# One-hot matmuls for the first gather and the last combine of a routed expert layer, and row numbers made in a copied last body

## The chip, the cores and the metric

The kernel runs on one NeuronCore of a Trainium2 chip. The metric is the device time of one execution in microseconds (us), lower is better. Five engines work side by side, each through its own list of instructions: TensorE (PE; its weight loads are shown apart as PEld), VectorE (DVE), ScalarE (ACT), GpSimd (POOL) and SyncE (SP, which only issues transfers). They meet at semaphores.

## What is computed

A two-layer transformer trunk over 256 tokens of width 1024, all in float32: attention, memory cross-attention and a feed-forward part in each layer, every one followed by `x = LayerNorm(ALPHA * x + part(x))`. The change touches only the last feed-forward part, a mixture of 8 experts of inner width 3584, of which each token takes the best two:

```python
def moe_swiglu(x, router, w_gate, w_up, w_down):
    logits = (x @ router).astype(jnp.float32)
    top_vals, top_idx = lax.top_k(logits, TOP_K)          # TOP_K = 2
    gates = jax.nn.softmax(top_vals, axis=-1)
    combine = jnp.sum(one_hot(top_idx, N_EXPERTS) * gates[..., None], axis=-2)
    y = jnp.zeros_like(x)
    for e in range(N_EXPERTS):                             # 8
        y = y + combine[..., e:e + 1] * swiglu(x, w_gate[e], w_up[e], w_down[e])
    return y
h = layer_norm(ALPHA * h + moe_swiglu(...), ln_g[1, 2], ln_b[1, 2])
```

## The kernel before

**Weights in chunks.** Every weight matrix comes in chunks of 128 x 2048 floats (1 MB), issued by SP into a ring of raw tiles. ACT rounds a chunk into `w_hi` (the `copy` at L993), DVE takes the rest into `w_lo` (L1798 in the expert loop, L1344 before it), and PE multiplies with three products for each piece, `x_hi*w_hi`, `x_hi*w_lo`, `x_lo*w_hi` (L362 to L364), 12 matmuls a chunk in the expert loop. There are three slots for `w_hi` and `w_lo`: ACT may split chunk n + 3 only when PE has finished chunk n (`chunk_used`), and DVE follows ACT (`hi_made`), PE follows DVE (`lo_made`).

**The expert loop.** An expert is one job of a hardware loop on each of PE, ACT, DVE and POOL, `n_rounds * 8` jobs (one round with these inputs). A job has 42 chunks, numbered c = 0 to 41: c = 0 to 27 make, for seven column blocks j, the gate (two chunks, bank `eg`) and the up product (two chunks, bank `eu`); c = 28 to 41 are the down product, in two halves of seven chunks (`ed0`, `ed1`). Beside them ACT does SiLU of a gate (L1282, at c%4 = 1), DVE multiplies it with the up product (L1790, c%4 = 3), PE transposes the result in the next block (L771), and ACT and DVE split the transposed tile (`eT_hi` at L993, `eT_lo` at L1812, c%4 = 2). ACT copies each finished half of `y` out of PSUM at c = 34 and c = 41 and issues its store to `y_rows` in HBM (L1293).

**Rows of tokens.** An expert works on at most 128 tokens. `place` holds each token's place in each expert, `pick` (L1724) is its one-hot form, 2 x 128 x 128. A matmul with `pick` makes the token numbers (L716), DVE turns them into integers (`got_i`), POOL gathers these rows of `x_rows` from HBM with an indirect transfer (L955), and PE turns the gathered tile (L726) before ACT and DVE split it into `xe_hi` and `xe_lo` (L1738). For the first expert all this stands ahead of the loop; for the next ones it is done inside the job before (index at c = 4, turn at c = 32).

**The end.** After the loop POOL gathers, for each half of the width, each of two token tiles and each of the two choices, 128 rows of `y_rows` into `y_got` (L964, 8 gathers), and DVE adds them, scaled by `g1` or `g2`, to X (L1831), makes the statistics (L1834) and does the last LayerNorm (L1837 to L1858). The row numbers for these gathers (`row_i`, L1752 to L1768), the gates (L1769 to L1771) and `X *= ALPHA` (L1778) are made by DVE ahead of the loop.

**Order.** Everything is ordered by hand: each engine runs the statements of its block in the order in which they are written, and waits block what stands behind them on the same engine.

Of the kernel before, what the change touches and what calls it, by code (L numbers as in the profile page):

```python
# [31 lines left out]
def trunk(nc, x, mem, ln_g, ln_b, mem_wq, mem_wkv, mem_wo, ab_w_in, ab_sinks, ab_w_out,  # L32
# [74 lines left out]
    with ExitStack() as ctx:  # L107
# [13 lines left out]
        def take(name, shape, dt=F32):  # L121
            size = 4
            for s in shape[1:]:
# [78 lines left out]
                   for i in range(2)] for t in range(TB)] for half in range(2)]  # L202
        raw_exp = [raw[(N0 + i) % NRAW] for i in range(NRAW)]
# [13 lines left out]
        for name, shape, dt in (  # L217
# [7 lines left out]
                ("row_i11", [P, 1], U32)):  # L225
# [10 lines left out]
            small[n] for n in ("token_no", "got_i", "mine", "nth", "late"))  # L236
        row_i = [[small[f"row_i{t}{i}"] for i in range(2)] for t in range(TB)]
# [32 lines left out]
        C_INDEX, C_TURN = 4, 4 * EJ + 4  # L270
# [71 lines left out]
        def _(pe):  # L342
# [368 lines left out]

            def index(tag, job):
# [18 lines left out]
            index("iA", None)  # L731
            pe.wait_ge(sem("x_got"), 16)
            turn("xA", None)
            pe.wait_ge(sem("rounds_made"), 1)
            n_rounds = pe.value_load(rounds[0:1, 0:1], min_val=1, max_val=2)
            before = [list(claims), list(signals)]
            with pe.Fori(0, n_rounds * NE) as job:
                start = list(claims)
                for c in range(EC):
# [4 lines left out]
                    if c == C_INDEX:  # L744
                        pe.wait_ge(sem("picked"), job + 2)
                        index("iB", job)
                    if c < 4 * EJ:
                        j, q = c // 4, c % 4
                        key, b = (f"eg{j}", j % 2) if q < 2 else (f"eu{j}", 2 + j % 2)
# [4 lines left out]
                    else:  # L754
                        i, q = divmod(c - 4 * EJ, EK // CK)
                        if q == 0:
                            claim(pe, f"ed{i}", 4 + i, job, signal=False)
                        if i == 0:

                            wait_emptied(pe, f"et{q}", job)  # L760
# [3 lines left out]
                    if c % 4 == 1 and 1 <= c // 4 <= EJ:  # L764
# [4 lines left out]
                        d = claim(pe, f"et{j}", b, job)  # L769
# [4 lines left out]
                    if c == C_TURN:  # L774

                        pe.wait_ge(sem("x_got"), 16 * job + 32)
                        turn("xB", job)
            assert [a - b for a, b in zip(claims, before[0])] == JOB_CLAIMS
            assert [a - b for a, b in zip(signals, before[1])] == JOB_SIGNALS

# [55 lines left out]
        def _(pool):  # L836
# [132 lines left out]
            pool.wait_ge(sem("y_filled"), 16 * 2 * (NE * P // SEQ))  # L969
# [3 lines left out]
            pool.wait_ge(sem("index_made"), 1)  # L973
            get_x()
            pool.wait_ge(sem("rounds_made"), 1)
# [12 lines left out]
        def _(act):  # L988
# [274 lines left out]
            with act.Fori(0, n_rounds * NE) as job:  # L1263
                for c in range(EC):
# [32 lines left out]
                    else:  # L1297
# [3 lines left out]
                        with act.Else():  # L1301
                            act.nop()
# [584 lines left out]
```

## Time and profile before

| | us |
|---|---|
| median of 3 runs | 1739.4 (1738.62 to 1739.58) |
| the profiled execution | 1737.09 |
| its span in the trace | 1735.3 |
| PE busy | 1648.1 |
| DVE busy | 1274.5 |
| ACT busy | 1069.5 |
| POOL busy | 102.9 |

The expert layer takes the second half of the span, from about 740 us on. The page says how busy each engine is; who waits for whom in a stretch is read from the timeline of that stretch, and what sets the end from the chain of work that ended last.

### The profile page before, as it was taken

The numbers are of one execution on the slowest core, as the hardware profiler recorded it, in microseconds if no ns is written. First come the engines' busy times: TensorE is split into PE (matmuls) and PEld (weight loads), VectorE is DVE, ScalarE is ACT, GpSimd is POOL, SyncE is SP. The second block draws the span as 40 slices with busy tenths as digits, with TensorE's granted clock in tenths as the row PEclk, the third lists the DMA queues.
The fourth block names the chain that finished last, engine by engine and source line by source line (L and its number), as shares of the span: only waits on it lengthen the run. The fifth ranks groups of instructions, "written<-read, shape, count | busy, mean of one in ns | idle before, by whom it ended". The sixth has DMA issues, their size and how long they took to land.

```text
span 1735.3 us, 21609 instructions
## 1 busy us (share of the span) xinstructions
PE 1648.1 (95%) x7704; PEld 1355.7 (78%) x7704; DVE 1274.5 (73%) x1080; ACT 1069.5 (62%) x951; POOL 102.9 (6%) x124
## 2 busy tenths in 40 slices
PE   7998988999999998799999999999999999999994
PEld 6787777888787787578878788788788788787883
DVE  4564746445655664588889799898898898898996
ACT  4575444434344544367777777777777777777772
POOL 2000110000101210100000000000000000000002
PEclk9998999999999999889999999999999999999997
DMA  9423915545555444389999999999999999999993
GB/s 317 169 73 121 309 56 193 182 158 194 193 185 171 131 149 143 121 287 365 376 376 374 372 374 363 376 377 371 368 380 362 381 364 377 379 360 379 373 366 108
DMA packets 238097, 480.56 MB, mean 277 GB/s; under 512 B 8224, under 2 KB 11328, under 8 KB 238048
## 3 DMA queue, kind: packets, MB, share of 16 engines
q1 hardware_dynamic: 229456, 454.06, 73.5%
q0 software_dynamic: 6288, 21.63, 4.0%
q10 hardware_dynamic: 2304, 4.20, 0.6%
q8 instruction: 32, 0.52, 0.1%
q14 instruction: 17, 0.14, 0.0%
HBM read 473.54 MB, written 10.51 MB: 279 GB/s over the span
## 4 chain that ended last, share of the span: by engine, by line
PE 81%; DVE 8%; ACT 7%; issue 3%; DMA 1%; ACTq 1%; POOL 0%; POOLq 0%; DVEq 0%
PE bank L362 25%; PE bank L364 24%; PE bank L363 24%; ACT w_hi L993 3%; DVE w_lo L1798 2%; PE bank L406 2%; DVE w_lo L1344 1%; PE bank L771 1%; PE bank L651 1%; DVE X L1381 1%; DVE X L1390 1%; ACT y L993 1%; PE bank L503 1%; PE bank L501 1%; ACT L1282 1%
## 5 line engine op out<-in xcount | busy, mean ns | idle before, releaser
L993 ACT ACTIVATE w_hi<-raw 128x2048 fp32r<-128x2048 f32 (+1 forms) x385 | 730.7, 1904 | 301.2 <-PE bank L364 286.2
L1798 DVE TENSOR_TENSOR w_lo<-raw,w_hi 128x2048 fp32r<-128x2048 f32 x285 | 647.2, 2291 | 114.1 <-ACT w_hi L993 102.3
L362 PE MATMUL bank<-w_hi,xe_hi 128*128 128x512 f32 x896 | 356.9, 398 | 5.8 <-DVE w_lo L1798 5.0
L364 PE MATMUL bank<-w_hi,xe_lo 128*128 128x512 f32 x896 | 350.2, 391 | 0.0
L363 PE MATMUL bank<-w_lo,xe_hi 128*128 128x512 f32 x896 | 349.9, 391 | 0.0
L1344 DVE TENSOR_TENSOR w_lo<-raw,w_hi 128x2048 fp32r<-128x2048 f32 (+1 forms) x95 | 210.9, 2223 | 158.6 <-ACT w_hi L993 158.4
L362 PE MATMUL bank<-w_hi,xT_hi 128*128 128x512 f32 (+1 forms) x560 | 216.8, 387 | 8.4 <-DVE w_lo L1344 5.2
L364 PE MATMUL bank<-w_hi,xT_lo 128*128 128x512 f32 (+1 forms) x560 | 214.4, 383 | 0.0
L363 PE MATMUL bank<-w_lo,xT_hi 128*128 128x512 f32 (+1 forms) x560 | 214.2, 383 | 0.0
L362 PEld LDWEIGHTS bank<-w_hi,xe_hi 128*128 128x128 f32 x896 | 168.8, 188 | 45.8 <-DVE w_lo L1798 11.5
L364 PEld LDWEIGHTS bank<-w_hi,xe_lo 128*128 128x128 f32 x896 | 168.6, 188 | 36.2
L363 PEld LDWEIGHTS bank<-w_lo,xe_hi 128*128 128x128 f32 x896 | 168.9, 189 | 33.2
L362 PE MATMUL bank<-w_hi,eT_hi 128*128 128x512 f32 x448 | 176.9, 395 | 2.2 <-DVE w_lo L1798 2.2
L364 PE MATMUL bank<-w_hi,eT_lo 128*128 128x512 f32 x448 | 174.7, 390 | 0.0
L363 PE MATMUL bank<-w_lo,eT_hi 128*128 128x512 f32 x448 | 174.4, 389 | 0.0
L362 PEld LDWEIGHTS bank<-w_hi,xT_hi 128*128 128x128 f32 x560 | 106.3, 190 | 29.6 <-issue 10.0
L364 PEld LDWEIGHTS bank<-w_hi,xT_lo 128*128 128x128 f32 x560 | 106.2, 190 | 20.7
L363 PEld LDWEIGHTS bank<-w_lo,xT_hi 128*128 128x128 f32 x560 | 106.4, 190 | 19.7
L1798 DVE TENSOR_TENSOR w_lo<-raw_more,w_hi 128x2048 fp32r<-128x2048 f32 x48 | 109.9, 2290 | 12.0 <-ACT w_hi L993 10.2
L993 ACT ACTIVATE w_hi<-raw_more 128x2048 fp32r<-128x2048 f32 x48 | 92.1, 1919 | 21.7 <-PE bank L364 21.7
L362 PEld LDWEIGHTS bank<-w_hi,eT_hi 128*128 128x128 f32 x448 | 84.1, 188 | 22.2 <-DVE w_lo L1798 5.6
L364 PEld LDWEIGHTS bank<-w_hi,eT_lo 128*128 128x128 f32 x448 | 84.1, 188 | 17.9
(264 smaller groups left out, 1617.2 us busy)
## 6 DMA issues: line engine op xcount, KB each, us to landing
raw<-in_moe_w_gate_dram SPq DMA_DIRECT2D x96, 1024.0 KB, 7.1
raw<-in_moe_w_up_dram SPq DMA_DIRECT2D x96, 1024.0 KB, 7.1
raw<-in_moe_w_down_dram SPq DMA_DIRECT2D x96, 1024.0 KB, 7.6
raw<-in_mem_wkv_dram SPq DMA_DIRECT2D x16, 1024.0 KB, 5.0
raw_more<-in_moe_w_up_dram SPq DMA_DIRECT2D x16, 1024.0 KB, 7.1
raw_more<-in_moe_w_gate_dram SPq DMA_DIRECT2D x16, 1024.0 KB, 6.6
raw_more<-in_moe_w_down_dram SPq DMA_DIRECT2D x16, 1024.0 KB, 7.8
raw<-in_c_w_in_dram SPq DMA_DIRECT2D x12, 1024.0 KB, 5.1
```

Source lines behind the costliest of these rows:

```text
L362: nc.tensor.matmul(d, xh, hi[:, k, :], start=(first and k == 0), stop=False)
L363: nc.tensor.matmul(d, xh, lo[:, k, :], start=False, stop=False)
L364: m = nc.tensor.matmul(d, xl, hi[:, k, :], start=False, stop=(last and k == n - 1))
L406: m = nc.tensor.transpose(dst[k // 2][:, c:c + P], src[:, t, k * P:(k + 1) * P], ident[:, :])
L501: nc.tensor.matmul(d[:, 0:P], qT[:, 0:P], kT[:, 0:P], start=True, stop=True, skip_group_check=True)
L503: m = nc.tensor.matmul(d[:, P:TRI], qT[:, P:SEQ], kT, start=True, stop=True, skip_group_check=True)
L651: m = nc.tensor.matmul(d[:, t * MDH:(t + 1) * MDH], PT_t[i % 2][:, mb * SEQ + t * P:mb * SEQ + (t + 1) * P], MV[:, mb, i * MDH:(i + 1) * M ...
L771: m = nc.tensor.transpose(d[:, q * P:(q + 1) * P], e_h[j % 2][:, q * P:(q + 1) * P], ident[:, :])
L993: return nc.scalar.activation(dst, src, ACT.Copy)
L1282: nc.scalar.activation(e_g[j % 2][:, :], bank_of(f"eg{j}")[:, :], ACT.Silu)\
L1344: tt(w_lo[c % NSPL][:, 0:n], raw[c % NRAW][:, 0:n], w_hi[c % NSPL][:, 0:n].bitcast(F32), ALU.subtract).then_inc(lo_made, 1)
L1798: tt(w_lo[s][:, :], raw_exp[r][:, :], w_hi[s][:, :].bitcast(F32), ALU.subtract).then_inc(lo_made, 1)
```

## The change

Five things are done.

1. **First expert's rows by matmul.** Instead of index, gather and turn ahead of the loop, PE multiplies X (still in SBUF) with `pick`: 16 matmuls of 128 columns give the transposed rows at once (`pick_rows`).
2. **The last job is a copy.** The loop runs `last = 8 * rounds - 1` jobs, and the last expert is a second, straight copy of the body (`expert(last, "z")`). The tests on the last three chunks' splits go away.
3. **Last expert's result by matmul.** In the copy PE transposes `pick` (c = 4), DVE copies it to `pickT` (c = 5), and PE multiplies it with `y` half by half (`combine`, after c = 37 and after c = 41); DVE adds that to X from PSUM (`add_last`). The last expert's `y` isn't stored. The eight gathers from HBM now concern only the other experts: they are issued as soon as the last but one expert is stored and the row numbers are made, and DVE adds them at c = 12, 16, 20 and 24 (`add_got`). A token's share from the last expert gets weight 0 there and its gate in `w_fin`.
4. **Row numbers, gates and `X *= ALPHA`** move from ahead of the loop into the copy, at c = 2 and c = 6.
5. **SiLU's table** is loaded by ACT at the top of every expert, by hand.

The core of the diff:

```diff
+        C_GOT = {12 + 4 * n: (n // TB, n % TB) for n in range(2 * TB)}
+        C_INDEX, C_TURN, C_COMBINE = 4, 4 * EJ + 4, 4 * EJ + EK // CK + 2
# TensorE
+            def pick_rows(tag):
+                for half in range(2):
+                    d = claim(pe, f"{tag}{half}", half)
+                    for q in range(4):
+                        k = 4 * half + q
+                        for t in range(TB):
+                            m = nc.tensor.matmul(d[:, q * P:(q + 1) * P], X[:, t, k * P:(k + 1) * P],
+                                                 pick[:, t, :], start=(t == 0), stop=(t == 1),
+                                                 skip_group_check=True)
+                    m.then_inc(filled[half], 1)
             pe.wait_ge(sem("picked"), 1)
-            index("iA", None)
-            pe.wait_ge(sem("x_got"), 16)
-            turn("xA", None)
-            with pe.Fori(0, n_rounds * NE) as job:
+            pick_rows("xA")
+            def combine(half, job):
+                for t in range(TB):
+                    d = claim(pe, f"c{half}{t}", 2 * half + t, job)
+                    if t == 0:
+                        pe.wait_ge(sem(f"y_made{half}"), job + 1)
+                    nc.tensor.matmul(d[:, :], pickT[:, t * P:(t + 1) * P], y[:, half * W:(half + 1) * W],
+                                     start=True, stop=True, skip_group_check=True)\
+                        .then_inc(filled[2 * half + t], 1)
+            def expert(job, z):
                     if c == C_INDEX:
                         pe.wait_ge(sem("picked"), job + 2)
-                        index("iB", job)
+                        if z:
+                            d = claim(pe, "pT", 5, job)
+                            for t in range(TB):
+                                m = nc.tensor.transpose(d[:, t * P:(t + 1) * P], pick[:, t, :], ident[:, :])
+                            m.then_inc(filled[5], 1)
+                        else:
+                            index("iB", job)
-                    if c == C_TURN:
+                    if c == C_TURN and not z:
                         turn("xB", job)
+                    if z and c in (C_COMBINE, EC - 1):
+                        if c == C_COMBINE:
+                            pe.wait_ge(sem("pickT_made"), 1)
+                        combine(int(c == EC - 1), job)
+            with pe.Fori(0, last) as job:
+                expert(job, "")
+            expert(last, "z")
# GpSimd
-                        for r in range(NE * P, 2 * NE * P, SEQ):
+                        for r in range((NE - 2) * P, 2 * NE * P, SEQ):
-            pool.wait_ge(sem("index_made"), 1)
-            get_x()
-            with pool.Fori(0, n_rounds * NE) as job:
-                pool.wait_ge(sem("index_made"), job + 2)
+            with pool.Fori(0, last) as job:
+                pool.wait_ge(sem("index_made"), job + 1)
                 get_x()
             for half in range(2):
-                pool.wait_ge(sem(f"y_kept{half}"), 16 * (n_rounds * NE) + 16)
+                pool.wait_ge(sem(f"y_kept{half}"), 16 * last + 16)
                 get_y(half)
# ScalarE
+            def expert(job, z):
+                nc.scalar.preload_act_table_set("silu_and_others")
-                        act.dma_start(y_rows[i][bass.ds(job * P, P), :], y[:, i * W:(i + 1) * W])\
-                            .then_inc(sem(f"y_kept{i}"), 16)
-                    if c < EC - NSPL:
+                        if not z:
+                            act.dma_start(y_rows[i][bass.ds(job * P, P), :], y[:, i * W:(i + 1) * W])\
+                                .then_inc(sem(f"y_kept{i}"), 16)
+                    if c < EC - NSPL or not z:
                         w_split()
-                    else:
-                        with act.If(job < n_rounds * NE - 1):
-                            w_split()
# VectorE, ahead of the loop
-            indexed("iA", None)
-            (row numbers, gates, X *= ALPHA)
# VectorE
+            def row_numbers():
                 (the statements of before, and)
+                dve.wait_ge(sem("rounds_made"), 2)
+                link(nc.vector.tensor_scalar(fin[:, :], most[:, :], float(NE * P), -float(P), ALU.mult, ALU.add))
+                link(nc.vector.tensor_scalar(is_fin[:, :, :], nth[:, :, :], fin[:, 0:1], None, ALU.is_ge))
+                link(tt(late[:, :, :], nth[:, :, :], is_fin[:, :, :], ALU.mult))
+                link(tt(nth[:, :, :], nth[:, :, :], late[:, :, :], ALU.subtract))
+            def gate_weights():
                 (the statements of before, and)
+                for i, g in enumerate((g1, g2)):
+                    ins = tt(w_fin[:, i, :], g[:, :], is_fin[:, i, :], ALU.mult)
+                link(ins)
+                for i, g in enumerate((g1, g2)):
+                    tt(g[:, :], g[:, :], w_fin[:, i, :], ALU.subtract)
+                link(tt(w_fin[:, 2, :], w_fin[:, 0, :], w_fin[:, 1, :], ALU.add))
+            def add_got(half, t):
+                xs = X[:, t, half * W:(half + 1) * W]
+                for i, g in enumerate((g1, g2)):
+                    dve.wait_ge(sem(f"y_got{half}{t}{i}"), 16)
+                    link(nc.vector.scalar_tensor_tensor(
+                        out=xs, in0=y_got[half][t][i][:, :], scalar=g[:, t:t + 1], in1=xs,
+                        op0=ALU.mult, op1=ALU.add))
+            def add_last(half, job):
+                for t in range(TB):
+                    xs = X[:, t, half * W:(half + 1) * W]
+                    b = wait_filled(dve, f"c{half}{t}", job)
+                    link(nc.vector.scalar_tensor_tensor(
+                        out=xs, in0=b[:, :], scalar=w_fin[:, 2, t:t + 1], in1=xs,
+                        op0=ALU.mult, op1=ALU.add))
+                    ins = nc.vector.bn_stats(stats[:, t, half, :], xs)
+                link(ins)
+            def expert(job, z):
+                    if c == C_INDEX + 1 and z:
+                        b = wait_filled(dve, "pT", job)
+                        link(copy(pickT[:, :], b[:, 0:TB * P]))
+                    if z and c == 2:
+                        row_numbers()
+                    if z and c == 6:
+                        gate_weights()
+                    if z and c in C_GOT:
+                        add_got(*C_GOT[c])
+                    if z and c == C_COMBINE + 1:
+                        add_last(0, job)
+            with dve.Fori(0, last) as job:
+                expert(job, "")
+            expert(last, "z")
+            add_last(1, last)
```

## Rows read from the trace of the kernel before

**Rows 1.** The page: busy us (share of the span) and instructions.

```profile
PE 1648.1 (95%) x7704; PEld 1355.7 (78%) x7704; DVE 1274.5 (73%) x1080; ACT 1069.5 (62%) x951; POOL 102.9 (6%) x124
```

**Rows 2.** One expert's stretch: us, busy PE, PEld, DVE, ACT, POOL, clock, DMA share, GB/s.

```profile
868.50:989.60 121.10, 120.13 (x545) 98.47 (x545) 105.30 (x62) 91.88 (x63) 2.68 (x1) 1.00 1.02 373
```

**Rows 3.** Chain of work before the loop: start us, us, what.

```profile
733.81 1.03 PE bank L716 x4
...
735.86 4.43 DMA x_got<-x_rows,got_i
...
741.49 0.61 ACT xe_hi L993
...
743.13 0.79 PE bank L362
```

**Rows 4.** Timeline of PE (start us, us): turn, clock's rise, two float32 products.

```profile
740.33 1.97 PE L726 MATMUL bank<-ident,x_got 128*128 128x128 f32 x8 [5.51 <-DMA x_got<-x_rows,got_i]
...
746.27 0.63 PE L363 MATMUL bank<-w_lo,xe_hi 128*128 128x512 f32 x1
...
747.26 0.40 PE L363 MATMUL bank<-w_lo,xe_hi 128*128 128x512 f32 x1
...
112.47 0.39 PE L519 MATMUL bank<-P,tri_ge 128*128 128x128 f32 x2
...
686.87 3.72 PE L651 MATMUL bank<-MV,PT 128*128 128x256 f32 x16
```

**Rows 5.** Timeline of ACT, top of the last expert.

```profile
1594.75 1.28 ACT L993 ACT_TABLE_LOAD   x1
...
1597.98 1.28 ACT L1282 ACT_TABLE_LOAD   x1
1599.27 0.60 ACT L1282 ACTIVATE e_g<-bank 128x512 f32<-128x512 f32 x1
1599.77 3.71 ACT L993 ACTIVATE w_hi<-raw 128x2048 fp32r<-128x2048 f32 x2
```

**Rows 6.** Timelines of DVE and PE, same place.

```profile
1601.71 4.50 DVE L1798 TENSOR_TENSOR w_lo<-raw,w_hi 128x2048 fp32r<-128x2048 f32 x2 [1.02 <-ACT w_hi L993]
...
1603.22 0.50 PE L716 MATMUL bank<-token_no,pick 128*128 128x1 f32 x4
1604.06 0.50 PE L362 MATMUL bank<-w_hi,xe_hi 128*128 128x512 f32 x1 [0.34 <-DVE w_lo L1798]
```

**Rows 7.** Timeline of DVE: moved row numbers' first and last, X *= ALPHA, one add's pair.

```profile
735.82 0.17 DVE L1752 TENSOR_TENSOR mine<-hot,place 128x16 f32<-128x16 f32 x1
...
737.29 0.34 DVE L1329 CAST row_i<-nth 128x1 uint32<-128x1 f32 x4
...
745.84 1.22 DVE L1778 TENSOR_SCALAR X<-X 128x2048 f32<-128x2048 f32 x1
...
1708.66 1.53 DVE L1831 SCALAR_TENSOR_TENSOR X<-y_got,g,X 128x512 f32<-128x512 f32 x2
```

**Rows 8.** By source line: ns min/median/max, first and last start us; gathers and splits.

```profile
L955 POOL DMA_INDIRECT x_got<-x_rows,got_i x9: 1015/2687/2692, 735.9 to 1615.4; - x9
...
DMA to landing us min/median/max: 4.4/9.0/9.3
...
L1798 DVE TENSOR_TENSOR w_lo<-raw,w_hi x285: 2282/2293/2296, 749.9 to 1703.7; 128x2048 fp32r<-128x2048 f32 x143
```

**Rows 9.** Chain of work at the end.

```profile
1712.66 0.61 ACT y L993
...
1713.42 2.02 DMA y_rows<-y
...
1720.00 3.90 DMA y_got<-y_rows,row_i
...
1724.78 0.71 DVE stats L1834
...
1725.51 0.29 DVE mean_var L1837 x2
```

More of the change, by code:

```diff
@@ L236, in trunk @@
             small[n] for n in ("token_no", "got_i", "mine", "nth", "late"))
+        fin, is_fin, w_fin, last_job = (small[n] for n in ("fin", "is_fin", "w_fin", "last"))
         row_i = [[small[f"row_i{t}{i}"] for i in range(2)] for t in range(TB)]
@@ L1775, in _ @@
             split(N0 + NSPL - 1)
-            dve.wait_ge(sem("x_kept"), 16 * TB)
-            link(nc.vector.tensor_scalar(X[:, :, :], X[:, :, :], ALPHA, None, ALU.mult))
-            n_rounds = dve.value_load(rounds[0:1, 0:1], min_val=1, max_val=2)
-            with dve.Fori(0, n_rounds * NE) as job:
+            dve.wait_ge(sem("rounds_made"), 2)
+            last = dve.value_load(last_job[0:1, 0:1], min_val=NE - 1, max_val=2 * NE - 1)
+            def row_numbers():
+                tt(mine[:, 0, :, :], hot1[:, :, :], place[:, :, 0:NE], ALU.mult)
+                link(tt(mine[:, 1, :, :], hot2[:, :, :], place[:, :, 0:NE], ALU.mult))
+                link(nc.vector.tensor_reduce(nth[:, :, :], mine[:, :, :, :], AX_X, ALU.add))
+                link(nc.vector.tensor_scalar(late[:, :, :], nth[:, :, :], float(P), float((NE - 1) * P),
+                                             ALU.is_gt, ALU.mult))
+                link(tt(nth[:, :, :], nth[:, :, :], late[:, :, :], ALU.add))
+                for i in range(2):
+                    for t in range(TB):
+                        ins = nc.vector.tensor_scalar(late[:, i, t:t + 1], best_f[:, t, i:i + 1], float(P),
+                                                      -float(P + 1), ALU.mult, ALU.add)
+                link(ins)
+                link(tt(nth[:, :, :], nth[:, :, :], late[:, :, :], ALU.add))
+                dve.wait_ge(sem("rounds_made"), 2)
+                link(nc.vector.tensor_scalar(fin[:, :], most[:, :], float(NE * P), -float(P), ALU.mult, ALU.add))
+                link(nc.vector.tensor_scalar(is_fin[:, :, :], nth[:, :, :], fin[:, 0:1], None, ALU.is_ge))
+                link(tt(late[:, :, :], nth[:, :, :], is_fin[:, :, :], ALU.mult))
+                link(tt(nth[:, :, :], nth[:, :, :], late[:, :, :], ALU.subtract))
+                for i in range(2):
+                    for t in range(TB):
+                        ins = copy(row_i[t][i][:, :], nth[:, i, t:t + 1])
+                ins.then_inc(sem("rows_made"), 1)
@@ new lines, in gate_weights @@
+            def gate_weights():
+                dve.wait_ge(sem("gap_exp"), 1)
+                link(nc.vector.tensor_scalar(g1[:, :], gap[:, :], 1.0, None, ALU.add))
+                link(nc.vector.reciprocal(g1[:, :], g1[:, :]))
+                link(tt(g2[:, :], g1[:, :], gap[:, :], ALU.mult))
+                for i, g in enumerate((g1, g2)):
[4 more added lines that the diff above has]
+                link(tt(w_fin[:, 2, :], w_fin[:, 0, :], w_fin[:, 1, :], ALU.add))
+                dve.wait_ge(sem("x_kept"), 16 * TB)
+                link(nc.vector.tensor_scalar(X[:, :, :], X[:, :, :], ALPHA, None, ALU.mult))
@@ L1822, in _ @@
                         nc.vector.nop().then_inc(emptied[fillings["iB"][0]], 1)
-                    if c == C_TURN:
+                    if c == C_TURN and not z:
                         turned("xB", job)
-            for half in range(2):
-                for t in range(TB):
-                    xs = X[:, t, half * W:(half + 1) * W]
-                    for i, g in enumerate((g1, g2)):
-                        dve.wait_ge(sem(f"y_got{half}{t}{i}"), 16)
-                        link(nc.vector.scalar_tensor_tensor(
-                            out=xs, in0=y_got[half][t][i][:, :], scalar=g[:, t:t + 1], in1=xs,
-                            op0=ALU.mult, op1=ALU.add))
-                    ins = nc.vector.bn_stats(stats[:, t, half, :], xs)
@@ L1835, in _ @@
-            link(ins)
+                    if z and c == 2:
[7 more added lines that the diff above has]
+            with dve.Fori(0, last) as job:
+                expert(job, "")
+            expert(last, "z")
+            add_last(1, last)
             for t in range(TB):
```

99 lines of the change are left out of this document (39 added, 60 removed).

## The prediction, made before the changed kernel was run

> **What bounds the kernel now.** I read the page first: PE is busy 1648.1 of 1735.3 us [rows 1]. Then the stretch of one expert: 121.10 us, PE busy 120.13, all at full clock, DVE 105.30, ACT 91.88, the transfers at a share of 1.02 and 373 GB/s [rows 2]. So inside an expert PE is the bound, DVE has 15.8 us of room in 121, and the reader is to see that the room is small: every 2.72 us (12 matmuls of 0.227) DVE owes one split of 2.29 us [rows 8] and it also has the small steps of the body. Last I read the two places where PE does not run: ahead of the loop and after it, by the chain of work [rows 3, 9].
>
> **The sum's frame.** Durations are those of the profiled execution, 1737.09 us, of which 1735.3 is the span. The median of the runs is 1739.4, so 2.3 us more; I add that at the end.
>
> **1. The start.** Before, PE begins the index product at 733.81, the gather's issue is at 735.86 and takes 4.43 us, the turn starts at 740.33, ACT's copy at 741.49, the first weight matmul is at 743.13 [rows 3]. Then PE is at half clock: its matmuls show 0.63 us until 746.27 and 0.40 from 747.26 on [rows 4]. Starts were 0.427 apart instead of 0.227, nine of them, so 9 x 0.20 = 1.8 us more. Full-speed start before: 743.13 + 1.8 = 744.9.
> After, PE starts `pick_rows` at 733.8, as `pick` is made by the same instructions. Its 16 products of 128 columns are float32, which shows as two records each: at full clock one such product (L519) comes 0.22 us after the one before it. At half clock eight records of 128 columns took 1.97 us with their tail, about 0.22 each [rows 4], so 0.44 a product: 16 x 0.44 = 7.0 us if the clock stays at 1.2 GHz, 3.5 us if it were full. In the trace the clock rose 4 us after the weight matmuls began (743.13 to about 747) [rows 3, 4]; I take 4.5 us. These make 10 products, six remain at 0.22: 733.8 + 4.5 + 1.3 = 739.6. Its first half is done at 737.3, and the way from there through ACT and DVE took 743.13 - 741.49 = 1.64 us [rows 3], so this is covered by the second half. DVE isn't late: without the row numbers and gates its split stands at about 735 to 737.3. First weight matmul 739.7, at full clock. Gain 5.2 us. Ends: no rise before 740.7 and chunk 0 also at half clock, 744.9 - 742.5 = 2.4; an early rise, 6.2.
>
> **2. The tops of the experts.** ACT loads a table twice at each top: 1594.75 before a copy, 1597.98 before the first SiLU, 1.28 each [rows 5]. The new load by hand stands where the first is, so only the second goes. It sits between a split and SiLU that both could run (their inputs are older), so all later ACT work comes 1.3 us earlier. What PE gets of it is less: DVE's next split waited 1.02 us for ACT and started at 1601.71, and PE, done with the index product 0.36 us after 1603.22, started chunk 4 only at 1604.06 with a first matmul 0.1 longer [rows 6]. That is 0.48 + 0.1 = about 0.55 us. The stalls at chunks 2 and 3 (0.4 each) come from the y copy and the first load, which stay. Seven tops (the first expert has no such stall): 7 x 0.5 = 3.6 us. Between 0 and 7 x 1.3 = 9.1; the row at chunk 4 is direct, so 3.6. The tests on the last three splits cost nothing visible, PE goes over the loop's edge without a gap.
>
> **3. The copied body on PE.** Taken away: the turn at c = 32, eight records of 0.109 at full clock, 0.87; the index, 0.36. Added: two transposes, 0.22, and `combine(0)` after c = 37: two float32 products of 512 columns. L651 with 256 columns shows 16 records in 3.72 us, 0.22 a record after the tail is taken off [rows 4]; 512 columns take twice that, four records: 1.7 us. Net +0.7 us, all on PE's path. `combine(0)` waits for nothing (y's first half is copied at c = 34, `pickT` is made at c = 5).
>
> **4. The copied body on DVE.** Here the moved work lands, and PE waits behind it.
> Row numbers: 735.82 to 737.63 [rows 7], 1.8 us, plus four new linked steps of 0.2: 2.6 us, at c = 2. The `pickT` copy 0.5 at c = 5. Gates: three linked steps, 0.6, four more 0.7, `X *= ALPHA` 1.22 [rows 7]: 2.5 us, at c = 6. Four pairs of adds, 1.53 each [rows 7], in all 6.2. Together 11.8 us. Taken away: `got_i` and two `xe_lo`, 1.5, at other places.
> What of it reaches PE: I go through the last expert with its own starts. Without the load, chunk 4 starts at 1603.4, chunk 5 at 1606.2, chunk 6 is due at 1609.3 (with the transposes of block 0). DVE splits chunks 4 and 5 until 1605.2, then 2.6 of row numbers to 1607.8, then the product at c = 3 (0.9 with its wait) to 1608.7, then chunk 6 to 1611.0: PE waits 1.7 + 0.1. Chunks 7 to 9 recover it (2.72 against 2.23). At c = 6 DVE ends chunk 9 at 1618.5, `eT_lo` at 1619.1, gates and X at 1621.6, the product at 1622.4, chunk 10 at 1624.7; PE is there at 1622.5: 2.2 us. From then on a group of four chunks takes PE 11.35 us and DVE 10.5, and each pair of adds makes the latter 12.0: the first is half taken by what DVE is ahead (0.4), the other three cost about 0.6 each. Sum 1.8 + 2.2 + 0.4 + 1.8 = 6.2 us. Ends: 2 us if DVE is further ahead than I think, 11.8 if all is serial. PE has no other work in these waits. `add_last(0)` at c = 38 stands behind the last split and costs nothing.
> Queues: POOL's eight gathers now go out beside the weights. Row numbers are there at about 17 us into the expert; a gather beside the splits takes POOL 2.69 us and lands 9.0 us after its issue [rows 8]. The first pair is there 15 us later, DVE asks for it 23 us later; each further pair has twice its 5.4 us. They add 2.1 MB, and 1 MB of loads and stores goes away: 2.8 us more of transfer time at 373 GB/s, against chunks that land 7 us after an issue made about 14 us ahead. Hidden. If that cover were gone, 2.8 us.
>
> **5. The end.** Before: y's copy at 1712.66, store 2.02 us, the gathers, the last landing after 3.90, the statistics, and 1725.51 for the means [rows 9]. After: copy done at 1713.3, `combine(1)`'s first product 0.85 and its tail 0.2, DVE add 0.7, statistics 0.7, the second pair behind it 1.4: 1713.3 + 1.05 + 2.8 + 0.1 = 1717.3 (the second product, at 1715.2, is no longer waited for). ACT's table load for the root is as early as before. Gain 8.2 us. The rest (LayerNorm, store) is the same. Even at half clock `combine(1)` would cost only 0.85 more.
>
> **Sum.** -5.2 - 3.6 + 0.7 + 6.2 - 8.2 = -10.1 us: 1727.0 beside the profiled 1737.09, 1729.3 beside the median.
>
> **Rivals.**
> A. *DVE takes the gain back in full.* The copied body runs DVE-bound from c = 2 to c = 24 and all 11.8 us appear: +5.6 on the forecast, 1734.9. For: 10.5 of 11.35 us are taken before anything is added. Against: the waits of DVE for ACT in the rows (0.2 to 0.8 at nearly each split) are room.
> B. *Better than forecast:* the clock rises early and DVE's work is half hidden: -1 - 4, 1724.
> C. *The table is still loaded twice,* since the load by hand names a set and the copy may ask for another: +3.6, 1732.9. Against: after SiLU's load all copies of an expert run without a new one, so that set holds the copy.
> D. *Slower: the gathers hold VectorE.* In the last expert, c = 3 to c = 16, eight gathers of 2.69 us of POOL work stand beside a DVE with no room. If each blocked DVE for its time, 8 x 2.69 = 21.5 us would all lie on PE's path: 1729.3 + 21.5 = 1750.8. It decides the sign from 1.3 us a gather on, and beyond 0.2% from 1.7 us. Against: nine gathers ran beside the loop's splits, and of 285 splits the longest is 2.296 us against a median of 2.293, while POOL's issue grew from 1.015 to 2.69 [rows 8]: POOL is what waits.
> The Trainium skill (SBUF — State Buffer, section "Who interferes with whom") says that DVE and GpSimd share a port pair as an exclusive lock, and that issue order decides which of the two is blocked. By that rule D is possible; the trace shows only the blocking of POOL.
>
> **Chances.** Forecast, within 3 us: 0.50. A 0.17 (a third of it within 0.2%), B 0.12, C 0.07, D and anything of its size 0.06, a mixture that ends near no change 0.08. Two runs of this kernel can be told apart by about 0.2%, 3.5 us. Faster by more: 0.50 + 0.11 + 0.12 + 0.07 = 0.80; within: 0.06 + 0.08 = 0.14; slower: 0.06. The range takes in A, B and C: 1723.5 to 1736.5.
>
> **What would show it.** First weight matmul near 739.7 and no matmul at 0.63 after it; one table load for each top, chunk 4 without a wait; in the last expert PE waits for DVE's `w_lo` near chunks 6 and 10, about 2 us each, then under 1 us after chunks 15, 19, 23, 27; splits of 2.29 us there too; the means about 4 us after y's last copy starts. I am wrong if DVE waits for `y_got` inside the body, if splits grow, or if PE's clock falls to half in its waits at chunks 6 and 10, which would cost 1.7 us or more for each fall.

## The result, and the profile after

The changed kernel takes 1727.2 us (median of 4 runs, 1726.87 to 1728.62) where the kernel before took 1739.3 beside it: ratio 0.9933, 95% interval 0.9915 to 0.9950. The profiled execution took 1726.87, its span is 1724.8 (before 1735.3), so 10.5 us shorter. Forecast: a median of 1729.3 (range 1723.5 to 1736.5), 10.1 us less than before; by the medians it is 12.1 us less, by the two profiled executions 10.5. The page of the changed kernel, against [rows 1]:

```profile
PE 1653.1 (96%) x7722; PEld 1357.9 (79%) x7722; DVE 1276.7 (74%) x1091; ACT 1058.0 (61%) x941; POOL 103.2 (6%) x124
```

PE is busy 5 us longer in a span 10.5 us shorter: work went onto PE, and idle time went out at both ends. Where the 10.5 us are:

| part | before | after | difference | forecast |
|---|---|---|---|---|
| until `pick` is made (its start) | 733.27 | 734.55 | +1.3 | 0 |
| `pick` to the first weight matmul, with what PE's half clock adds behind it | 9.86 + 1.8 | 5.88 | -5.8 | -5.2 |
| first expert | 119.8 | 119.84 | 0 | 0 |
| six more experts in the loop | 121.10 each | 120.48 each | -3.7 | -3.1 |
| last expert, first weight matmul to the last copy of `y` | 121.32 | 126.99 | +5.7 | +6.4 |
| last copy of `y` to the means | 12.85 | 4.85 | -8.0 | -8.2 |

(The forecast's 3.6 for seven tops is here 3.1 for six and 0.5 in the last expert, whose rest is +0.7 and +6.2.)

Timeline of PE at the start (start us, us, what, idle time before it), against [rows 3, 4]:

```profile
735.09 5.46 PE L723 MATMUL bank<-pick,X 128*128 128x128 f32 x32 [0.87 <-DVE pick L1766]
740.43 0.49 PE L366 MATMUL bank<-w_hi,xe_hi 128*128 128x512 f32 x1
740.77 0.39 PE L367 MATMUL bank<-w_lo,xe_hi 128*128 128x512 f32 x1
```

The two stretches there (us, busy PE, PEld, DVE, ACT, POOL, granted clock, DMA share, GB/s):

```profile
735.00:740.00 5.00, 4.91 (x29) 4.91 (x30) 3.25 (x8) 0.60 (x1) 0.00 (x0) 0.65 0.40 117
740.00:745.00 5.00, 5.00 (x25) 4.16 (x25) 3.08 (x3) 3.40 (x3) 0.00 (x0) 1.00 0.47 180
```

The 16 products (two records each) start 0.54 us after `pick`, and the weight matmuls follow without a gap. The first is 0.49 us long and the next 0.39: the 0.63 of [rows 4] is gone. The clock's way back to 2.4 GHz now lies under `pick_rows` (0.65 in the first stretch, 1.00 in the second).

Timeline of ACT at a top in the loop: one load where [rows 5] shows two.

```profile
984.12 1.28 ACT L1306 ACT_TABLE_LOAD   x1
...
985.41 1.92 ACT L1034 ACTIVATE w_hi<-raw 128x2048 fp32r<-128x2048 f32 x1
987.24 0.58 ACT L1325 ACTIVATE e_g<-bank 128x512 f32<-128x512 f32 x1
```

Timeline of DVE in the last expert, right behind the row numbers (1596.76 to 1599.42): the SiLU product and the next split.

```profile
1599.33 0.68 DVE L1867 TENSOR_TENSOR e_h<-bank,e_g 128x512 f32<-128x512 f32 x1
1600.24 2.29 DVE L1875 TENSOR_TENSOR w_lo<-raw_more,w_hi 128x2048 fp32r<-128x2048 f32 x1 [0.23 <-ACT w_hi L1034]
```

Timeline of PE in the last expert, the matmuls that waited (chunk 6, the transposes, chunks 10, 20, 24, 28):

```profile
1602.59 0.50 PE L366 MATMUL bank<-w_hi,xe_hi 128*128 128x512 f32 x1 [1.31 <-DVE w_lo L1875]
...
1613.97 0.65 PE L803 MATMUL bank<-ident,e_h 128*128 128x128 f32 x4 [0.21 <-DVE e_h L1867]
...
1616.41 0.50 PE L366 MATMUL bank<-w_hi,xe_hi 128*128 128x512 f32 x1 [1.79 <-DVE w_lo L1875]
...
1645.52 0.50 PE L366 MATMUL bank<-w_hi,xe_hi 128*128 128x512 f32 x1 [0.30 <-DVE w_lo L1875]
...
1657.50 0.50 PE L366 MATMUL bank<-w_hi,xe_hi 128*128 128x512 f32 x1 [0.27 <-DVE w_lo L1875]
...
1669.48 0.50 PE L366 MATMUL bank<-w_hi,eT_hi 128*128 128x512 f32 x1 [0.34 <-DVE w_lo L1875]
```

From the start of one matmul to the next, less the usual 0.227, the waits cost a little more (the first matmul after one shows 0.50 instead of 0.39): 1.47, 0.36, 2.00, 0.45, 0.43 and 0.50, and 0.1 more behind each of the last three. The granted clock stays at 1.00 behind all of them.

By source line (ns min/median/max, first and last start), one group of DVE's splits over the whole loop and the eight gathers of the last expert, against [rows 8]:

```profile
L1875 DVE TENSOR_TENSOR w_lo<-raw_more,w_hi x48: 2280/2293/2296, 754.0 to 1704.0; 128x2048 fp32r<-128x2048 f32 x48
...
L1006 POOL DMA_INDIRECT y_got<-y_rows,row_i x8: 957/1899/3032, 1599.7 to 1614.2; - x8
...
DMA to landing us min/median/max: 5.5/7.4/8.4
```

And the end, on ACT, PE and DVE, against [rows 9]:

```profile
1710.17 0.60 ACT L1034 ACTIVATE y<-bank 128x512 f32<-128x512 f32 x1 [6.24 <-PE bank L368]
1710.92 1.96 PE L758 MATMUL bank<-y,pickT 128*128 128x512 f32 x4 [0.78 <-ACT y L1034]
1712.12 0.75 DVE L1851 SCALAR_TENSOR_TENSOR X<-bank,w_fin,X 128x512 f32<-128x512 f32 x1 [3.10 <-PE bank L758]
1712.91 0.69 DVE L1854 BATCH_NORM_STATS2 stats<-X 128x6 f32<-128x512 f32 x1
1713.52 0.73 DVE L1851 SCALAR_TENSOR_TENSOR X<-bank,w_fin,X 128x512 f32<-128x512 f32 x1
1714.29 0.69 DVE L1854 BATCH_NORM_STATS2 stats<-X 128x6 f32<-128x512 f32 x1
1715.02 0.28 DVE L1915 BATCH_NORM_AGGREGATE mean_var<-stats 128x2 f32<-128x12 f32 x2
```

Store and gather are gone; two products and DVE's four steps stand in their place.

### The profile page after: what moved, and what is told of

Read it like the earlier page. It is cut to its first block, busy times and chain, and to the rows that moved or that the text cites. A ratio compares the mean times of both kernels' runs of the same rounds, so it can differ in the third digit from the quotient of the medians.

```text
span 1724.8 us, 21526 instructions
## 1 busy us (share of the span) xinstructions
PE 1653.1 (96%) x7722; PEld 1357.9 (79%) x7722; DVE 1276.7 (74%) x1091; ACT 1058.0 (61%) x941; POOL 103.2 (6%) x124
## 4 chain that ended last, share of the span: by engine, by line
PE 80%; DVE 10%; ACT 5%; issue 3%; DMA 1%; ACTq 0%; DVEq 0%; SPq 0%
PE bank L366 24%; PE bank L368 24%; PE bank L367 24%; DVE w_lo L1875 3%; ACT w_hi L1034 3%; PE bank L410 2%; DVE w_lo L1386 1%; PE bank L803 1%; PE bank L655 1%; DVE X L1423 1%; DVE X L1432 1%; PE bank L507 1%; DMA raw<-in_ab_w_in_dram 1%; PE bank L505 1%; ACT y L1034 1%
## 5 line engine op out<-in xcount | busy, mean ns | idle before, releaser
L366 PEld LDWEIGHTS bank<-w_hi,xT_hi 128*128 128x128 f32 x560 | 106.6, 190 | 29.7 <-issue 10.1
```

What stands on the lines that cost most here:

```text
L366: nc.tensor.matmul(d, xh, hi[:, k, :], start=(first and k == 0), stop=False)
```

## The experiments

The theory is the forecast's sum: a gain at the start, at the tops and at the end, and a loss in the last expert that comes from DVE's moved steps. The rivals that the chip was asked about: the gathers (D), something else in the tops than the table, something else in the last expert than DVE. Each ratio is to the kernel before on the same chip (medians 1738.4 to 1738.7 us); three kernels were run only once and have none. "Start distance" below is from the first weight matmul of one expert to that of the next; the last expert is taken to the start of the last copy of `y`, in the changed kernel 1710.17 - 1583.18 = 127.0.

### The gathers are not the loss

Run e7_no_gathers, the changed kernel without the eight gathers:

```diff
                 pool.sem_inc(sem("y_asked"), 1)
-                get_y(half)
 ...
-                    dve.wait_ge(sem(f"y_got{half}{t}{i}"), 16)
-                        out=xs, in0=y_got[half][t][i][:, :], scalar=g[:, t:t + 1], in1=xs,
+                        out=xs, in0=(eT_lo, read as 512 floats), scalar=g[:, t:t + 1], in1=xs,
```

> The changed kernel without the eight gathers from y_rows; VectorE does the same adds from another tile, so the other experts' shares are left out of the result. Theory (the gathers are hidden and don't hold VectorE): the last expert takes 127.0 us as before, its waits at chunks 6, 10, 20, 24 and 28 unchanged within 0.1 us. Rival (the gathers' work on GpSimd holds VectorE or their transfers delay weights): the last expert gets shorter by 0.5 us or more.

Measured: 1726.9 us (one execution). The last expert takes 126.8 instead of 127.0, and its waits are 1.47, 2.01, 0.50, 0.44 and 0.44, as with the gathers. Rival D falls. In the changed kernel POOL's issue of a gather took 0.96 to 3.03 us, and no split of the loop took over 2.296. The Trainium skill (SBUF — State Buffer, section "Who interferes with whom") lets the order of issue decide which of DVE and GpSimd is blocked; here only GpSimd's instructions were seen to get longer.

### The tables

Run e3_table_only, the kernel before with the load at the top alone:

```diff
             with act.Fori(0, n_rounds * NE) as job:
+                nc.scalar.preload_act_table_set("silu_and_others")
                 for c in range(EC):
```

> The kernel before with the table load at the top of each job as its only edit. Theory (the second load reaches PE only through the split of chunk 4): an expert takes 120.5 us instead of 121.1 from top to top, the wait at chunk 4 is gone, those at chunks 2 and 3 stay; seven tops give 4.3 us, 1735.0 us beside 1739.3. Rival (the gain from top to top in the changed kernel comes from the tests on the last three splits, which this kernel keeps): an expert stays at 121.1 us and the time at 1739.

Measured: 1734.8, ratio 0.998 (0.9971 to 0.9990), start distances 120.58 instead of 121.10: 0.52 a top. The step "0.5 a top" holds. The changed kernel has 120.48 (120.53 in another execution, a1_changed, below); the 0.1 that is left comes from something else in the loop, and no run tells what.

Run e4_table_once, the changed kernel with one load ahead of the loop and none in it:

```diff
+            nc.scalar.preload_act_table_set("silu_and_others")
             def expert(job, z):
-                nc.scalar.preload_act_table_set("silu_and_others")
                 for c in range(EC):
```

> The changed kernel with the table loaded once, ahead of the loop, and no load inside it. Theory (the first load of a top delays the split of chunk 3 and PE waits 0.36 us and 0.1 us for it): an expert takes 120.0 us instead of 120.5, the wait at chunk 2, which comes from the y copy, stays; seven tops, -3.2 us against the changed kernel. If the load also costs PE at chunk 2: up to -5. Rival (the wait at chunk 3 comes from the y copy too): no change.

Measured: 1724.1, ratio 0.9923 (0.9907 to 0.9940), start distances 119.97, so 0.51 less for each top, and 126.4 for the last expert. The profile shows no table load in the loop at all. The load that the change kept was worth as much as the one that it took away; of the two waits that the change had left at the tops, that at chunk 3 (0.36 us and 0.11 behind it) went with it, and that at chunk 2 (0.25 us and 0.11 behind it), which stands behind the copy of `y`, stayed.

### The last expert: DVE's steps, taken away, doubled, moved

Run e1_rows_early, row numbers, gates and `X *= ALPHA` out of the last expert and ahead of the loop:

```diff
-                    if z and c == 2:
-                        row_numbers()
-                    if z and c == 6:
-                        gate_weights()
...
+            row_numbers()
+            gate_weights()
             with dve.Fori(0, last) as job:
```

> The changed kernel with the row numbers, the gates and X *= ALPHA put back ahead of the loop, behind the split of the third chunk. Theory (VectorE's moved steps are what PE waits for in the last expert): the waits at chunks 6 and 10 of the last expert (1.5 and 2.0 us, with the 0.2 and 0.4 beside them) go, the last expert takes 123.0 us instead of 126.97 from its first matmul to its last, and ahead of the loop the 5.1 us of VectorE find 1.2 us of idle time, then what the splits are ahead, so chunk 3 of the first expert may come up to 1.5 us late. Net -2.5 to -4 us against the changed kernel, about 1723.5 to 1724.5 us. Rival (the last expert is longer by what a first pass through copied code costs, or by the gathers beside it): it stays at 126 to 127 us, and the time is that of the changed kernel plus 0 to 1.5 us.

Measured: 1727.4, ratio 0.9939 (0.9923 to 0.9956), no gain, where 1723.5 to 1724.5 was expected. The last expert did what was expected: 1710.46 - 1587.44 = 123.0 instead of 127.0. But the first expert takes 124.52 instead of 119.84. Timelines of DVE (first and last moved step, the next split) and of PE:

```profile
743.30 0.17 DVE L1801 TENSOR_TENSOR mine<-hot,place 128x16 f32<-128x16 f32 x1
...
747.07 1.23 DVE L1837 TENSOR_SCALAR X<-X 128x2048 f32<-128x2048 f32 x1
...
748.53 2.29 DVE L1875 TENSOR_TENSOR w_lo<-raw,w_hi 128x2048 fp32r<-128x2048 f32 x1 [0.23 <-DVE X L1837]
...
750.87 0.61 PE L366 MATMUL bank<-w_hi,xe_hi 128*128 128x512 f32 x1 [2.80 <-DVE w_lo L1875]
...
751.28 0.63 PE L367 MATMUL bank<-w_lo,xe_hi 128*128 128x512 f32 x1
```

The stretches (columns as above):

```profile
747.50:750.00 2.50, 0.57 (x3) 0.15 (x1) 2.27 (x2) 2.18 (x2) 0.00 (x0) 1.00 0.19 66
750.00:752.50 2.50, 1.63 (x4) 1.30 (x5) 2.50 (x4) 0.02 (x1) 0.00 (x0) 0.72 0.25 26
752.50:755.00 2.50, 2.50 (x8) 1.97 (x7) 2.50 (x2) 0.00 (x0) 0.00 (x0) 0.60 0.95 362
```

5.0 us of steps stand in one piece ahead of chunk 3's split. PE waits 2.8 us (its matmul starts 2.95 later than 0.227 behind the last one), and then some nine matmuls come 0.43 apart instead of 0.227: 1.8 us more. 2.95 + 1.8 is the 4.7 that the first expert lost. Before, the row numbers and gates lay in DVE's wait for the gather [rows 3, 7], and `X *= ALPHA` (745.84) in its wait for ACT's split of chunk 3, which began only when PE had gone through chunk 0 at half clock:

```profile
749.87 2.29 DVE L1798 TENSOR_TENSOR w_lo<-raw,w_hi 128x2048 fp32r<-128x2048 f32 x1 [2.81 <-ACT w_hi L993]
```

So they cost nothing; the change took both covers away.

Run e5_start_only, the start of the change alone, on the kernel before (`pick_rows`; the numbers, gates and `X *= ALPHA` behind the third split, since `X` must be whole until then):

```diff
-            index("iA", None)
-            pe.wait_ge(sem("x_got"), 16)
-            turn("xA", None)
+            pick_rows("xA")
```

> The kernel before with only the first expert's rows made by matmul; the row numbers, gates and X *= ALPHA stay ahead of the loop, behind the split of the third chunk. Theory (gather, turn and half clock in chunk 0 go; 16 products take 5.3 us): from pick to the first weight matmul 5.9 us instead of 9.9, that matmul at full clock, -5.8 us against before, less up to 1.5 us for the row numbers in front of the first splits: 1733.5 to 1735 us. Rival (the clock comes back only later, as it isn't the matmuls but the phase that decides): the first weight matmuls at half clock, -4 us or less.

Measured: 1737.1, ratio 0.9993 (0.9984 to 1.0003), where 1733.5 to 1735 was expected. From `pick` to the first weight matmul it is 735.16 to 741.09, 5.93 us, so `pick_rows` does here what it does in the changed kernel. The first expert then takes 123.89 instead of 119.8. Timelines of DVE and PE at chunk 3:

```profile
749.44 2.29 DVE L1804 TENSOR_TENSOR w_lo<-raw,w_hi 128x2048 fp32r<-128x2048 f32 x1 [1.15 <-issue]
...
751.79 0.50 PE L362 MATMUL bank<-w_hi,xe_hi 128*128 128x512 f32 x1 [2.23 <-DVE w_lo L1804]
```

The stretch behind it:

```profile
752.50:755.00 2.50, 2.50 (x9) 1.92 (x8) 2.50 (x2) 0.00 (x0) 0.00 (x0) 0.58 0.83 230
```

The same wait, the same fall of the clock to near 1.2 GHz behind it, and a third thing: 1.15 us in which DVE does nothing that the profile shows. What stands there in the code is the read of `rounds` into a register, behind a step that it has to wait for; in e1_rows_early, where the read stands earlier, it is 0.23 us at this place. No run moves the read alone.

Run e6_rows_twice, the row numbers made twice in the last expert:

```diff
                     if z and c == 2:
+                        row_numbers(first=True)
                         row_numbers()
```

> The changed kernel with the row numbers made twice in a row at c = 2 of the last expert (the second time over the same tiles), 2.5 us more of VectorE. Theory (VectorE is the bound there, one for one): PE's wait at chunk 6 grows from 1.5 to 4.0 us; if PE's clock falls to half after so long a wait, as it did in the first expert of the kernel with early row numbers, 1.8 us more. Rival (the wait at chunk 6 has another cause, for instance ScalarE's splits): it stays at 1.5 us.

Measured: 1732.0 (one execution); the last expert takes 131.3, 4.35 more. Timeline of PE, its waits near chunk 6:

```profile
1603.61 0.66 PE L803 MATMUL bank<-ident,e_h 128*128 128x128 f32 x4 [1.99 <-DVE e_h L1870]
...
1606.06 0.63 PE L366 MATMUL bank<-w_hi,xe_hi 128*128 128x512 f32 x1 [1.79 <-DVE w_lo L1878]
```

The stretches:

```profile
1604.00:1606.00 2.00, 0.27 (x3) 0.03 (x1) 2.00 (x2) 0.06 (x1) 1.70 (x2) 1.00 0.45 129
1606.00:1610.00 4.00, 3.94 (x10) 3.15 (x11) 4.00 (x3) 0.00 (x0) 3.39 (x3) 0.57 0.67 200
```

2.66 us more on DVE come through to PE in full (waits of 4.1 instead of 1.47), and 1.7 more from the clock. So with DVE already the late one, what was added to it cost PE as much again. The first 2.66 had cost 1.47, the rest was room.

Run e9_adds_late, the adds of the other experts' rows moved behind the busy stretch:

```diff
-        C_GOT = {12 + 4 * n: (n // TB, n % TB) for n in range(2 * TB)}
+        C_GOT = {33: (0, 0), 37: (0, 1), 39: (1, 0), 40: (1, 1)}
```

> The changed kernel with only the four pairs of adds moved, to c = 33, 37, 39 and 40 of the last expert. Theory (each pair costs PE what VectorE is short of in a group of four chunks): the waits of 0.45, 0.43 and 0.50 us (chunks 20, 24 and 28) go, with the 0.17 at chunk 16 and the slower first matmul behind each; those at chunks 6 and 10 stay; the last expert takes 125.1 us instead of 127.0. Rival (these waits come from the copied body's own splits): it stays at 127.0 us.

Measured: 1726.6 (one execution), the last expert 125.2; the waits at chunks 20, 24 and 28 are gone, 1.49 and 2.00 stay. The adds cost 1.8 us more where they stood than at their new place, where a wait of 0.2 us shows.

### Versions that use it

Run f1_spread. One load; row numbers in two parts, between the first splits; `X *= ALPHA` behind the third; gates at c = 33; adds at c = 36, 37, 39, 40; the register read ahead of all that:

```diff
             split(N0 + 1)
+            dve.wait_ge(sem("rounds_made"), 2)
+            last = dve.value_load(...)
+            row_numbers_1()
-            turned("xA", None)
+            turned("xA", None, between=row_numbers_2)
             split(N0 + NSPL - 1)
+            link(nc.vector.tensor_scalar(X[:, :, :], X[:, :, :], ALPHA, None, ALU.mult))
```

> The changed kernel with the table loaded once and VectorE's moved steps spread over its idle time: row numbers in two parts between the splits of the first rows, X *= ALPHA behind the third split, the gates at c = 33 of the last expert, the four pairs of adds at c = 36, 37, 39 and 40, and the register with the number of jobs read behind the first split. Theory (each step costs what it exceeds VectorE's idle time by): first weight matmul within 0.3 us of the changed kernel's after pick, first expert 120 us or less than 1 us more, tops 119.97 us apart, last expert 126.99 - 0.6 (table) - 4.0 (chunks 6 and 10) - 1.4 (the adds' waits) = 121.0 us: about 1717.5 us against 1727.2 for the changed kernel and 1724.1 with the table loaded once. Rival (the waits behind the adds are those of a copied body and stay): 1719 us or more.

Measured: 1718.35, ratio 0.9883 (0.9867 to 0.9900). First expert 119.79, start distances 119.96, last expert 1701.17 - 1580.78 = 120.4 instead of 127.0. PE sees none of the steps that in e1_rows_early cost it 4.7 us in the first expert: ahead of the loop only one piece of them now stands between two splits. The gates went to c = 33 and the register read forward in the same run, and no run separates these from the spreading.

What is left is ahead of the loop. The stretches of this kernel, while the routing is worked out:

```profile
720.00:725.00 5.00, 1.97 (x8) 1.57 (x8) 4.08 (x10) 1.49 (x4) 1.11 (x3) 0.72 0.19 79
725.00:730.00 5.00, 4.68 (x24) 2.79 (x24) 1.86 (x5) 4.98 (x5) 0.47 (x1) 0.60 0.94 255
730.00:735.00 5.00, 2.59 (x12) 2.41 (x12) 1.90 (x14) 0.87 (x2) 0.00 (x0) 0.75 0.95 307
```

PE waits for DVE's LayerNorm and routing, its granted clock falls to near half, and its small products, which all others wait for, then run at that. The next three versions put matmuls in whose result nobody reads. In f2_spread_busy they stand ahead of PE's waits for `taken` (5) and `pick` (3):

```diff
+            keep_busy(5)
             pe.wait_ge(sem("taken_made"), 1)
...
+            keep_busy(3)
             pe.wait_ge(sem("picked"), 1)
             pick_rows("xA")
```

> The kernel f1_spread with eight matmuls of 512 columns whose result nobody reads: five while PE waits for the experts' choice, three while it waits for pick. Theory (PE's clock is at half in this stretch because it was idle before): the places and the 16 products of the first rows run at full clock for more of their time; from the choice to the first weight matmul up to 2.9 us less. Rival (the clock stays at half whatever PE does there, or the added matmuls stand in front of the awaited ones): no gain, or up to 1 us more.

Measured: 1716.2, ratio 0.9871 (0.9855 to 0.9888). From `taken` to `pick` it is 1.84 us instead of 2.85, and from `pick` to the first weight matmul 5.76 instead of 5.94; but the clock doesn't hold: it is 0.81 and 0.85 in the stretches to 735 and 740, and `pick_rows` takes 5.47 us as before. The medians are 2.2 us apart, so these rows explain about half; ahead of `taken` this execution is 0.9 shorter, where nothing was changed. Then, in f3_busy_earlier, with the unread matmuls earlier too (14 ahead of the second half of the turn of the output of the last LayerNorm ahead of the experts, 6, 3). The 14 overwrite the part of X already turned, so this kernel routes and multiplies other values:

> The kernel f1_spread with unread matmuls of 512 columns in three waits of PE: 14 between the two halves of the turn of X ahead of the router (3.9 us of wait), 6 before the experts' choice is awaited, 3 before pick is. Theory (idle PE is what lowers its clock): the second half of that turn and the router's 24 products run at full clock, 0.9 + 1.8 us less than at half, beside the 1.0 us that the later ones gave; 1714.5 to 1715.5 us. Rival (PE's start after the wait sets nothing, or ScalarE's and VectorE's splits of the turned tile do): no more than the 2.2 us that f2_spread_busy gave, 1716.

Measured: 1714.7, ratio 0.9866 (0.9851 to 0.9881). Since its data was changed, f4_busy_kept has them write only the columns that are turned next:

```diff
+                    if key == "1n1" and t == 1:
+                        late = (columns of the second token tile in that bank)
+                        for _ in range(28):
+                            nc.tensor.matmul(late, mT_hi[:, 0, 0:P], mT_hi[:, 0, :], ...)
```

> The kernel f3_busy_earlier again, with its 14 unread 512-column matmuls ahead of the second half of the last turn replaced by 28 unread ones of 256 columns, which write only the columns of that bank that the turns write next, so that nothing that is still read is overwritten. It computes everything that the kernel before computes. Theory (what the start loses between 715 and 740 us is TensorE's granted clock, which falls when the engine has little to do while the other engines work out the routing): the granted clock stays at 1.00 in the stretch 715 to 740 us as in f3, the 32 products of the row selection take 3.8 to 4.0 us instead of 5.5, the first weight matmul starts at about 737.1, the rest of the loop is f1's, and the time is 1714 to 1715.5 us (f1: 1718.35; ratio to before about 0.9866). Rival (the time of f3 came from values that its overwritten bank changed, not from the clock): the start is f1's or f2's again and the time is 1716 to 1718.5.

Measured: 1714.8 (1714.39 to 1715.89), ratio 0.9864 (0.9848 to 0.9881), the shortest of the kernels that compute everything. Two stretches of it:

```profile
720.00:725.00 5.00, 4.42 (x35) 3.76 (x33) 4.26 (x11) 1.03 (x3) 0.40 (x1) 1.00 0.26 105
725.00:730.00 5.00, 3.65 (x29) 2.72 (x29) 2.96 (x8) 4.98 (x6) 1.19 (x3) 1.00 0.82 221
```

And the timeline of PE at the start:

```profile
733.48 3.84 PE L735 MATMUL bank<-pick,X 128*128 128x128 f32 x32
738.65 0.49 PE L366 MATMUL bank<-w_hi,xe_hi 128*128 128x512 f32 x1 [1.34 <-DVE xe_lo L1796]
```

From that LayerNorm's final step to `pick` it is 722.89 to 732.94, 10.05 us, where f1_spread takes 13.10: 3.05 us, of which 0.25 lie ahead of the router's products, 1.79 in these 24 (0.115 apart, where in f1_spread they were 0.213 apart at first) and 1.02 between `taken` and `pick`. After `pick` only 0.2 is gained (5.71 against 5.94): `pick_rows` is 1.6 us shorter, but then PE waits 1.34 for `xe_lo`. Timelines of ACT and DVE there:

```profile
735.57 0.60 ACT L1047 ACTIVATE xe_hi<-bank 128x512 fp32r<-128x512 f32 x1 [3.99 <-PE bank L735]
...
736.24 0.17 DVE L1810 TENSOR_TENSOR mine<-hot,place 128x16 f32<-128x16 f32 x1
...
737.72 0.69 DVE L1796 TENSOR_TENSOR xe_lo<-bank,xe_hi 128x512 fp32r<-128x512 f32 x1
```

`xe_hi`'s first half is ready at 736.17, and DVE does the first part of the row numbers until 737.7. So with `pick_rows` at full clock the place that was free in f1_spread is no longer free; no run moves the part from there. The medians differ by 3.6 us, so some 0.3 more than these rows show is open. The time of the run before was not a matter of its data; the first weight matmul stands later than expected (738.65 for 737.1) because in this execution that LayerNorm's final step began 1.6 us later (722.89, in f3_busy_earlier 721.31).

Run a1_changed, the changed kernel once more, as a measure of the runs:

> The changed kernel again, timed on the chip that also runs f3_busy_earlier, for the ratio between the two. 1727 us, 9 to 12 us above f3_busy_earlier by either theory.

Measured: 1726.6 (1725.87 to 1727.10), ratio 0.9935 (0.9921 to 0.9949), 12.0 us above f3_busy_earlier on the same chip. In its profiled execution `pick` starts at 733.40 and the first weight matmul at 739.03, and the last expert is 127.1 us long. So where `pick` comes depends on the execution by more than a microsecond, the body of the last expert by 0.1.

## Why the prediction was right

**Start.** The mechanism holds, 0.6 us undersized. From `pick`'s start at 733.27 the forecast had 6.4 us to the first weight matmul; it took 5.88, because the products began 0.54 us after `pick` and took 5.46. What was sized too large is the time at half clock: the forecast gave the products 4.5 us at half clock, and the 0.65 of the stretch from 735 to 740 leaves room for 3.5 of its 5 us. The 1.3 us by which `pick` came later is not the change's: in a1_changed, the same kernel, `pick` starts at 733.40, 0.1 after that of the kernel before. Most of it is the way from the last LayerNorm ahead of the experts to `pick`, 12.32 us before, 12.35 in a1_changed and 13.08 in the profiled execution of the changed kernel, with a granted clock of 0.80, 0.81 and 0.65 from 720 to 725; what sets it to the one or the other is open.

**Tops.** One table load went, with 0.52 us for each top: the term was right. With 120.48 the top-to-top distance is another 0.1 shorter, in no term. Of the rival C (table loaded twice) nothing is seen.

**Copied body on PE.** `combine(0)` was given 1.7 us; its four records begin at 1697.33 and the second weight matmul behind them at 1699.28, 1.95 us later, of which 0.23 are the first's: 1.72.

**Copied body on DVE.** The places were right: chunk 6 with 1.47 us for a forecast of 1.8, chunk 10 with 2.00 for 2.2, and the adds with 1.8 for 2.2 (0.45, 0.43, 0.50, 0.1 behind each, and 0.17 at chunk 16). Row numbers took 2.66 us for 2.6, gates and `X *= ALPHA` 2.62 for 2.5. In all the expert lost 0.7 us less than forecast. Rival A (all 11.8 us) falls, since the splits' waits for ACT were room, as the rows had said; but the doubled row numbers show how close it was: nothing was left of that room at chunk 6.

**End.** The gain was 8.0 us, for a forecast of 8.2.

**The other rivals.** D (the gathers hold VectorE) is refuted by e7_no_gathers. Rival B (1 us from an early rise of the clock, 4 us from DVE's work half hidden) came true for 0.6 us of the first and 0.7 of the second.

**What the sum didn't have.** It priced DVE's steps in their new place and took for granted that the old place was free to leave. e1_rows_early and e5_start_only show that with `pick_rows` the old place is no longer free either: there the steps cost 4.7 and 4.1 us (in e5_start_only the steps of before, with the register read). So of the gain at the start a part exists only because the steps went elsewhere. And behind a wait for DVE it named PE's clock only as a danger in the last expert, where it didn't fall.

**How close by merit.** 10.1 forecast against 10.5 in the profiled executions is closer than the terms were: start -0.6, tops -0.6, last expert -0.7 and end +0.2 are 1.7 us that the forecast lacked, and the late `pick` of this one execution took 1.3 back. By the medians it lacked 2.0.

## What to carry to other kernels

When a wait is removed, look at what lay in it: small steps that were free there need a new place, and the place is good when they stand one by one between the units that the bound engine waits for, not in one block; their sum alone says little (4.7 us in a block ahead of the loop, nothing when spread). And look again when PE gets faster in front of them, as f4_busy_kept shows. Price a wait of TensorE with the clock that may fall behind it. And where a table load is moved by hand, try one ahead of the loop and none in it before one for each turn.

## What the runs showed of the hardware that was not expected

- Behind an idle time of PE of 2.80 us (e1_rows_early), 2.23 us (e5_start_only) and two close ones of 1.99 and 1.79 us (e6_rows_twice) the granted clock fell to near half and 1.7 to 1.8 us were lost after the wait; behind 1.31 and 1.79 us in the changed kernel it stayed at 1.00 (2.4 GHz).
- Unread matmuls in PE's waits brought 3.05 us up to `pick`, by keeping the granted clock at 1.00 from 715 to 740 us.
- One load of SiLU's table ahead of a loop serves copies and SiLU of all experts; each load in it had cost PE 0.5 us a top, less than half of its own 1.28.
- Reading a value into one of DVE's registers behind a step that had to be waited for left, by the code, 1.15 us of nothing ahead of the loop (e5_start_only); placed earlier it was 0.23 (e1_rows_early). No run tests it alone.
